# Half of the prompt's attention moved into the expert stage, and expert rows summed by token

## The reference, cut to what matters

```python
mod = (silu(c) @ w_ada + b_ada)              # shift, scale, gate of both halves
h   = rms(x, g_pre1) * (1 + sc1) + sh1
q, k, v, p = split(h @ w_in)                  # 8 heads of 64; p goes to a pooling group
# stick-breaking attention, strictly causal, for each query over its keys
log_1mb = where(mask, log_sigmoid(-z), 0)
after   = cumsum(log_1mb, reverse=True) - log_1mb
w       = where(mask, exp(log_sigmoid(z) + after), 0);  o_a = w @ v
x   = x + gt1 * rms(concat(rms(o_a), rms(o_b)) @ w_out)
h2  = rms(x, g_pre2) * (1 + sc2) + sh2
# experts: for each token and each of 8 heads
s1, s2 = the two halves of (h2 @ w_query) times 128 keys each
v1, i1 = top_k(s1, 16);  v2, i2 = top_k(s2, 16)
best, sel = top_k(all sums v1 + v2, 16);  idx = i1 * 128 + i2 at sel
act = gelu(h2 . u_tab[idx])                   # 128 rows of u for a token
x   = x + gt2 * rms(sum over the 128 of softmax(best) * act * v_tab[idx])
```

## Time and profile before

| | |
|---|---|
| median of 3 runs | 3820.96 us (3818.93 to 3822.36) |
| the profiled execution, first to last instruction | 4199.6 us |
| modulation and projection | 0 to 381 us |
| attention | 381 to 665.8 us |
| output | 665.8 to 904.6 us |
| experts, from the first gather | 904.6 to 4199.6 us |
| bytes moved | 1245.5 MB, 1141.0 of them gathered rows |

### The profile page before, as it was taken

How to read it: one execution, slowest core, us unless ns; L and a number is a source line. 1 busy time by engine, 2 the same in 40 slices (tenths; PEclk the granted TensorE clock), 3 DMA queues, 4 the chain that set the end, 5 groups by cost and what they waited for, 6 DMA issues and landing times.

```text
span 4199.6 us, 38180 instructions
## 1 busy us (share of the span) xinstructions
PE 3314.8 (79%) x9348; PEld 1593.5 (38%) x9348; DVE 2313.6 (55%) x5821; ACT 950.0 (23%) x2161; POOL 2152.0 (51%) x2222
## 2 busy tenths in 40 slices
PE   8998989928777777877777777777777777887677
PEld 2454555513333333333333333333333333333222
DVE  2104552867755665555665655566555665556442
ACT  1003773312221221112112211211121121112111
POOL 0000300236566665666666666566666665666665
PEclk9999999969898898898888888888888888888888
DMA  9104102159999999999999999899999999999997
GB/s 357 64 15 126 32 19 113 61 188 352 344 357 359 353 359 354 347 368 343 341 359 347 350 356 344 332 354 355 360 347 358 358 357 348 343 363 358 361 362 303
DMA packets 365168, 1245.51 MB, mean 297 GB/s; under 512 B 52129, under 2 KB 57505, under 8 KB 362751
## 3 DMA queue, kind: packets, MB, share of 16 engines
q0 software_dynamic: 313504, 1141.02, 72.4%
q1 hardware_dynamic: 48852, 96.77, 6.6%
q10 hardware_dynamic: 2576, 5.10, 0.4%
HBM read 1220.34 MB, written 22.39 MB: 296 GB/s over the span
## 4 chain that ended last, share of the span: by engine, by line
PE 38%; issue 17%; another core or an unknown queue 9%; DVE 5%; DMA 4%; POOL 3%; ACT 1%; DVEq 0%; POOLq 0%; ACTq 0%; SPq 0%
PE ps_y L1692 33%; PE ps_q L950 5%; DMA urow<-in_u_tab,idx 3%; POOL urow L1473 2%; POOL vrow L1473 1%; DMA vrow<-in_v_tab,idx 1%; DVE urow L1612 1%; ACT diag L1580 1%; DVE aux L993 0%; PE ps_s L961 0%; DVE i L996 0%; DVE sel L996 0%; DVE i L992 0%; DVE aux L1029 0%
## 5 line engine op out<-in xcount | busy, mean ns | idle before, releaser
L1692 PE MATMUL ps_y<-vrow,diag 128*128 128x512 f32 (+1 forms) x4352 | 2220.8, 665 | 647.5 <-issue 329.9
L1612 DVE CUSTOM_DVE_ANT_0 urow<-urow,ps_h 128x1024 f32<-128x1024 f32 x1088 | 1299.8, 1220 | 1025.2 <-DMA urow<-in_u_tab,idx 865.6
L1692 PEld LDWEIGHTS ps_y<-vrow,diag 128*128 128x128 f32 (+1 forms) x4352 | 884.3, 209 | 1893.6 <-issue 1576.9
L1473 POOL DMA_INDIRECT vrow<-in_v_tab,idx x1088 | 1031.6, 948 | 785.7 <-issue 287.4
L1473 POOL DMA_INDIRECT urow<-in_u_tab,idx x1088 | 1030.7, 947 | 430.5 <-issue 282.8
L1580 ACT ACTIVATE diag<-const,wgt 128x128 f32<-128x128 f32 x1024 | 373.1, 396 | 1766.2 <-PE ps_y L1692 643.3
L950 PE MATMUL ps_q<-aux,w_q_sb 128*128 128x128 f32 x2048 | 271.7, 292 | 58.1 <-issue 49.4
L950 PEld LDWEIGHTS ps_q<-aux,w_q_sb 128*128 128x128 f32 x2048 | 263.9, 207 | 94.4 <-issue 93.2
L1293 POOL TENSOR_TENSOR xo<-xo,ot 128x1024 f32<-128x1024 f32 (+1 forms) x9 | 21.1, 2343 | 352.2 <-DVE ot L1249 352.2
L530 PE MATMUL ps_z<-hT,w_in_sb 128*128 128x512 f32 (+1 forms) x576 | 190.5, 491 | 4.6 <-DVE hT L448 4.6
L625 POOL MEMSET kTs<- 128x384 f32 x1 | 0.4, 418 | 322.7 <-POOLq L344 322.7
(11 more groups left out here) (181 smaller groups left out, 2341.3 us busy)
## 6 DMA issues: line engine op xcount, KB each, us to landing
ada<-in_w_ada SPq DMA_DIRECT2D x12, 2048.0 KB, 12.5
urow<-in_u_tab,idx POOLq DMA_INDIRECT x1088
vrow<-in_v_tab,idx POOLq DMA_INDIRECT x1088
w_in_sb<-in_w_in SPq DMA_DIRECT2D x8, 1024.0 KB, 17.9
w_q_sb<-in_w_query SPq DMA_DIRECT2D x8, 1024.0 KB, 14.3
x<-in_x_p ACTq DMA_DIRECT2D x8, 512.0 KB, 6.6
w_out_sb<-in_w_out SPq DMA_DIRECT2D x8, 512.0 KB, 7.0
xo<-in_x_p SPq DMA_DIRECT2D x8, 512.0 KB, 3.7
```

Source lines behind the costliest of these rows:

```text
L1473: nc.gpsimd.indirect_dma_start(ring[k % RING][:, :], None, A[table][:, :], bass.IndirectOffsetOnAxis(ap=places[:, col:col + 1], axis=0)).t ...
L1612: nc.vector.tensor_tensor_reduce(out=urow[k % RING][:, :], in0=urow[k % RING][:, :], in1=ps_h[:, :], scale=1.0, scalar=0.0, op0=ALU.mult, ...
L1692: last = nc.tensor.matmul(ps_y[0:rows, c], diag[s % DIAGS][:, 0:rows], vrow[k % RING][:, c], start=(s == 0), stop=(s == PH * width(n) - 1))
```

## The change

1. The attention stage keeps tokens 0 to 511 and the sample: 11 units for a pair in place of 27. The output stage keeps the sample's tile and four tiles; the sample's searches stand at 2 and 3 and, five of them, among the last steps.
2. Tokens 512 to 1023 are done by a new class `Front` inside the expert stage, in 102 steps ("spots"): 72 of attention (4 pairs by 18 spots for 16 units: a spot gives PE the values, "after" and next scores of neighbouring units, ACT four functions, DVE softplus and R), the others the norm, the product with w_out, residual and second norm. They stand in bodies 1 (3 in a head), 2, 3 and the start of 4 (4 in a head), behind a quad on PE and behind every fourth product on DVE. K, V, q, x, w_out and the outputs go through DRAM once more, about 24.6 MB by the shapes in the code.
3. Ten bodies instead of nine: body b gathers u for tile b and v for tile b - 1, in turn. A v gather fetches all 128 rows of one token (`idxT`, the indices transposed). Four tokens make a quad: 8 products on PE, each 128 rows by 32 columns of weights (`place`, a window with the token's weights in one column) by 512, into four groups of 32 PSUM partitions. The 128x128 diagonals and their copies on ACT are gone. The u ring has 6 buffers (`URING`), the v ring 8.
4. The search is cut in 17 pieces, one behind each product, and is that of two heads ahead (`g + 2`); PE's queries and scores are three heads ahead. One bank of PSUM (`ps_find`) serves queries and scores.

Small edits in the first stages merge semaphores. The core of the diff:

```diff
-    for qc in range(2):
-        top = 4 * qc + 3
-        for kb in range(top, -1, -1):
-            c0 = max(0, kb * P - qc * 512)
-            for h in range(2):
-                units.append(dict(h=h, bank=qc, kb=kb, c0=c0, c1=512, first=kb == top, diag=kb >= 4 * qc,
-                                  last=kb == 0, opens=kb == top and h == 0, closes=kb == 0 and h == 1))
+    top = EARLY - 1
+    for kb in range(top, -1, -1):
+        for h in range(2):
+            units.append(dict(h=h, bank=0, kb=kb, c0=kb * P, c1=HALF, first=kb == top, diag=True,
+                              last=kb == 0, opens=kb == top and h == 0, closes=kb == 0 and h == 1))
     for kb in (2, 1, 0):
-        units.append(dict(h=2, bank=2, kb=kb, c0=0, c1=P, first=kb == 2, diag=kb == 2, last=kb == 0,
...
     NTILE = len(tiles)
...
-    heads = {2: [0], 3: [1], 4: [2], 5: [3], 6: [4], 7: [5], 8: [6, 7]}
...
-                for h in heads.get(t, []):
-                    find.search(own, dve, dve_passed, 0, h)
+                if t == 2:
+                    search(0)
+                if t == 3:
+                    search(1)
+                    search(2)
...
             second(NTILE - 3)
-            find.search(own, dve, dve_passed, 0, PH - 2)
+            search(3)
             product(NTILE - 1)
-            find.search(own, dve, dve_passed, 0, PH - 1)
             second(NTILE - 2)
+            search(4)
             residual(NTILE - 1)
+            search(5)
             second(NTILE - 1)
+            search(6)
+            search(7)
...
+    def unit(self, m):
+        j, h = divmod(m % self.UNITS, 2)
+        kb = NT - 1 - j
+        diag = kb >= EARLY
+        c0 = P * (kb - EARLY) if diag else 0
+        return m // self.UNITS, j, h, kb, diag, c0, (c0 + P if diag else 0)
+
...
+        self.nc.tensor.matmul(self.z[m % 2][:, c0:HALF], self.kT[hr, P * kb:P * (kb + 1)], self.q[hr, c0:HALF],
+                              start=True, stop=True, skip_group_check=True).then_inc(self.z_done, 1)
+
+    def after(self, pe, m):
+        i, j, h, kb, diag, c0, lo = self.unit(m)
+        z = self.z[m % 2]
+        pe.wait_ge(self.sp_done, m + 1)
+        last = self.nc.tensor.matmul(z[:, c0:HALF], self.ntri, self.sp[m % 2][:, c0:HALF], start=False, stop=True,
+                                     skip_group_check=True)
+        if j and lo < HALF:
+            last = self.nc.tensor.matmul(z[:, lo:HALF], self.nones, self.R[h][(j - 1) % 2][:, lo:HALF], start=False,
+                                         stop=True, skip_group_check=True)
...
+        i, j, h, kb, diag, c0, lo = self.unit(m)
+        nc, s = self.nc, self.sp[m % 2][:, c0:HALF]
+        act.wait_ge(self.z_done, m + 1)
+        if m >= 2:
+
+            act.wait_ge(self.t_done, m - 1)
+        own.link(nc.scalar.activation(s, self.z[m % 2][:, c0:HALF], ACT.Abs))
+        own.link(nc.scalar.activation(s, s, ACT.Exp, scale=-1.0))
...
+        i, j, h, kb, diag, c0, lo = self.unit(m)
+        act.wait_ge(self.t_done, m + 1)
...
+        self.nc.scalar.activation(self.w[m % 2][:, c0:HALF], self.z[m % 2][:, c0:HALF], ACT.Exp)\
+            .then_inc(self.e_done, 1)
...
+        dve.wait_ge(self.l_done, m + 1)
+        soft = nc.vector.scalar_tensor_tensor(out=s[:, c0:HALF], in0=self.z[m % 2][:, c0:HALF], scalar=0.0,
+                                              in1=s[:, c0:HALF], op0=ALU.max, op1=ALU.add)
+        if diag:
...
+            new, old = self.R[h][j % 2], self.R[h][(j - 1) % 2]
+            fresh = HALF if j == 0 else lo
+            if fresh > c0:
+                own.add(nc.vector.tensor_copy(new[:, c0:fresh], s[:, c0:fresh]))
+            if fresh < HALF:
+                own.add(nc.vector.tensor_tensor(new[:, fresh:HALF], old[:, fresh:HALF], s[:, fresh:HALF], ALU.add))
...
+        def spot(g, j):
+
+            if g < PH:
+                return None
+            if g < 2 * PH:
+                return 3 * (g - PH) + j - 1 if j else None
+            p = 3 * PH + 4 * (g - 2 * PH) + j
+            return p if p < front.END else None
...
+                k, at = v_slot(n, i) % VRING, find.idxT[n % 2][:, t:t + 1]
...
+                nc.gpsimd.indirect_dma_start(vrow[k][:, :], None, A["v_tab"][:, :],
+                                             bass.IndirectOffsetOnAxis(ap=at, axis=0)).then_inc(v_full[k], 16)
+
+            for b in range(BODIES):
+                nu = PH * width(b) if b < NU else 0
+                nv = rows(b - 1) if b else 0
+                for i in range(max(nu, nv)):
+                    if i < nu:
+                        gather_u(b, i)
+                    if b == 1:
+                        if i % 2:
+                            gather_v(0, i // 2)
+                    elif i < nv:
+                        gather_v(b - 1, i)
...
-                        products(un, uh)
...
-                        find.search(own, dve, dve_passed, n + 1, h - 1)
...
+                    for k in range(w):
...
+                        if k == (1 if h == 0 else 2) and g:
+                            weights(g - 1)
+                        if b == 0:
...
+                        if g + 2 < HEADS and k + early < find.STEPS:
+                            find.search(own, dve, g + 2, k + early)
...
+                        if k % 4 == 3 and spot(g, k // 4) is not None:
+                            front.on_dve(dve, own, spot(g, k // 4))
...
+            def quad(n, c):
...
+                pe.wait_ge(placed, n * QUADS + c + 1)
+                for i in range(j):
+                    s = v_slot(n, j * c + i)
+                    pe.wait_ge(v_full[s % VRING], 16 * (s // VRING + 1))
                 for half in range(2):
...
-            def add_row(n, h, k):
-                rows = DEC if is_sample(n) else P
-                s = width(n) * h + k
-                pe.wait_ge(v_full[k % RING], filled(n, h, k))
-                pe.wait_ge(diag_ready, slots(n, h) + (k + 1))
-                for half in range(2):
-                    c = slice(512 * half, 512 * (half + 1))
-                    last = nc.tensor.matmul(ps_y[0:rows, c], diag[s % DIAGS][:, 0:rows], vrow[k % RING][:, c],
-                                            start=(s == 0), stop=(s == PH * width(n) - 1))
-                last.then_inc(v_used, 1)
...
+                    cols = slice(512 * half, 512 * (half + 1))
+                    for i in range(j):
+                        s = v_slot(n, j * c + i)
+                        last = nc.tensor.matmul(ps_y[QUADS * i:QUADS * (i + 1), cols],
+                                                place[:, z, i, MID - c:MID - c + QUADS], vrow[s % VRING][:, cols],
+                                                start=(c == 0), stop=(c == QUADS - 1))
+                        if half:
+                            last.then_inc(v_used, 1)
...
-            run(pe, lambda: None, body, lambda: None)
+                    g = head(b, h)
...
+                    for j in range(4):
...
+                        quad(b - 1, 4 * h + j)
+                        if j == 3 and g + 3 < HEADS:
+                            find.scores(pe, g + 3)
+                        if spot(g, j) is not None:
+                            front.on_pe(pe, spot(g, j))
...
+                            if h3 == 0 and j in (1, 2):
...
+                                find.queries(pe, g + 3)
```

More of the change, by code:

```diff
@@ new lines, in take_places, with by_slot @@
+    def take_places(self, dve, n, bank, v_used):
+        nc = self.nc
+        dve.wait_ge(self.idxT_tr, n + 1)
+        if n >= 2:
+            dve.wait_ge(v_used, v_slot(n - 1, 0))
+        nc.vector.tensor_copy(self.idxT[n % 2][:, 0:rows(n)], bank[:, 0:rows(n)]).then_inc(self.idxT_ready, 1)
+def by_slot(nc, n, bank, c0, tile, ident):
+    if not is_sample(n):
+        return nc.tensor.transpose(bank[:, c0:c0 + P], tile[:, :], ident)
+    for half in range(2):
+        p = slice(DEC * half, DEC * (half + 1))
+        last = nc.tensor.matmul(bank[p, c0:c0 + DEC], tile[p, 0:DEC], ident[p, p], start=True, stop=True,
+                                skip_group_check=True)
+    return last
@@ L1263, in second, with search @@
                                                op0=ALU.mult, op1=ALU.mult).then_inc(x1_scaled, 1)
+            def search(h):
+                for step in range(find.STEPS):
+                    find.search(own, dve, h, step)
             dve.wait_ge(S["prepared"], KC + 6)
@@ L1351, in _ @@
                     last.then_inc(ab_done, 1)
-                    if half == 0:
-                        for h in heads.get(t, [])[:1]:
-                            find.scores(pe, 0, h)
-                        for h in heads.get(t, [])[1:]:
-                            find.queries(pe, 0, h)
-                for h in heads.get(t, [])[1:]:
-                    find.scores(pe, 0, h)
+                    if half == 0 and t in (2, 3):
+                        find.scores(pe, t - 2)
+                        if t == 3:
+                            find.queries(pe, 2)
```

(37 more changed lines are left out.)

1140 lines of the change are left out of this document (760 added, 380 removed).

## The result

The changed kernel takes **3784.97 us** (median of 4 runs, 3776.31 to 3787.60) against 3821.66 (4 runs): ratio 0.9899, 95% interval 0.9885 to 0.9913. It is faster, as forecast, but by 37 us where 171 were forecast (3650).

The account below looks back on a forecast made before the run. It took the expert stage as near DMA-bound, attention and output as engine chains. First gather 683, gather-paced terms 2,524 and other terms 443 gave 3650 us timed; range 3575 to 3795, leaving out the chain and the fastest end.

Parts of the forecast that it names:

- first gather: End of attention and output: the expert stage's first gather at 683 us in place of 904.6, 222 us less.
- body 0 with its start: Expert stage's start: 7.4 us from first gather to first product, then 108 for 64 DVE products, u gathers alone.
- body 1: Second body of the expert stage: 8 heads of products, search pieces and 3 spots each on DVE, 290 us.
- bodies 2 to 8: 1,792 gathers at 1.45 us, 2598 profiled, plus 62 for moved transfers and 27 for PE; 2381 timed.
- last u gather to the end: Last body: 128 v gathers alone, 32 quads of 6.0 us, 192 profiled (170 timed), then 11 for last quad and norm.
- rows no cheaper: Rival, gathers of bodies 2 to 8: 1.489 us each, no gain, 70 us more (62 timed), 3715 to 3720; chance 0.15.
- quads one after another: Rival, PE in the expert stage: a quad takes 7.08 us, its products not side by side, about 3795; chance 0.11.
- Attention and output: Front stages: attention ends at 491.6 us; output's searches and other work bring the first gather to 683.
- To timed runs: Profile's 378.6 us excess put wholly in the gather stage: gather-paced terms times 0.885, 2852 to 2524 us.
- PE's load and the moved transfers: Expert bodies: 27 us for PE's overloaded heads and moved output steps, 62 us for moved transfers in DMA-bound bodies.
- chain exposed: Rival: DVE waits in order for ACT at 72 attention spots, up to 5 us each, 3830 to 3990; chance 0.12.
- DVE frees a u buffer after each product: Bodies 2 to 8: a buffer freed every 1.94 us, two gathers needing 2.9, so POOL's blocked time goes in part.

Follow-up runs that it names:

- second profile: The kernel before, unchanged, profiled again: 3819.2 us in its one execution, against 4199.6 in the profile the prediction was made from.
- block run: The changed kernel with 14 of a search's 17 pieces in one block behind a head's 13th product, not one behind each product: 3823.80 us.

## Why the prediction was wrong in size

From the experiments the 37 us are a sum of steps from kernel to kernel: the restructured stage **+25** (3848.71 - 3823.61, the runs of before beside it), half of the front gone **-233** (3848.71 to 3615.26), its work put into the bodies **+170**. The forecast of faster was right for the front's sake alone. By its own steps:

| step | forecast, timed | measured |
|---|---|---|
| first gather | 683 | 669 |
| body 0 with its start | 115 | 103 |
| body 1 | 290 | 314 |
| bodies 2 to 8 | 2299 + 55 + 27 = 2381 | 2449 |
| last u gather to the end | 170 + 11 = 181 | 250 |
| sum | 3650 | 3785 |

Three steps failed: the end, 69 us too low; the price of a gather in bodies 2 to 8, 46; and the moved work, 46 (22 in bodies 2 to 8, 24 in body 1). The first two rows came out 26 lower than forecast. That 3785 lies inside the stated 3575 to 3795 is luck: the upper part of that range stood for rows no cheaper and for quads one after another, not for what failed here.

*Attention and output*: right, 14 us too high. *Body 0*: DVE-bound as said (busy for 59 of 60 us between 700 and 760), 12 too high.

*To timed runs*: this step failed first, and the price of a gather with it. That the excess lay in the gather stage was right: the front of the second profile is as long as that of the first. But the prediction read room for the gathers from an execution at 352 GB/s, took half of it as gain (1.489 to 1.45) and put that through the factor 0.885, which made a gather 1.283 us. It is 335 / 256 = 1.309, and was 1.330 before (340.5 / 256), both at a DMA share of 1.01 or 1.02. That is 46 of the 68 in bodies 2 to 8. The sign was in the prediction: it computed 391 GB/s for a timed run and had 352 in view, and used that only against a rival.

*Rivals*: "rows no cheaper" was nearest for the rows, 1.489 x 0.885 = 1.318. That the DMA path was full was right; the level it was full at, 352, was that one execution's. The 358 GB/s that the Trainium skill gives for a core (DMA: Bandwidth & Descriptors, Specifications) agrees with the 352 of the first profile, and not with the 396 to 409 of the later ones; the rate there decides.

*The end*: mis-sized by 69. I priced the last body by the pace of gathers, 6.0 us for a quad profiled, while my own count of the v ring (22 of 23 us) held only for v gathers that come every 2.9 us. With v alone POOL issues them every 1.245, and eight buffers give 14.17 us for two quads, 7.1 each. The run with 14 buffers shows it: 60 us off, and 193 from the last u gather to the end where the forecast had 181.

*PE's load and the moved transfers*: the transfers were sized right (62 profiled, 55 timed, 57 measured). The 27 for PE was wrong in kind: with quads side by side PE is busy for 236 of 372 us in body 2. What costs is the order: in-order PE holds a spot behind a quad that waits for rows, and ACT, DVE and the u ring wait in line. That is the rival "chain exposed" in part. Its sign came: DVE's wait ahead of softplus is 2.6 us each (168.5 / 64), over the 2.4 that was to show the forecast wrong. Its price came only in part: 113 us over 72 attention spots, 1.6 each. The prediction set it aside because a spot has 11.6 us to the next; it left out that PE reaches the spot only behind the quad's wait, 9.03 us in the row above.

*Quads one after another*: did not happen. The run that forces it is 178 above the change, where the rival had 145; the sum is near by luck, since the rival had 84 for all heads and 35 for the end, and the run has 133 in bodies 1 to 4 and 13 in the last. The Trainium skill (TensorE: Matmul & The Clock Gate, Part 3) has three column tiles at 2.38 times; the run has four at 3.67.

*"DVE frees a u buffer after each product"* as a reason for cheaper rows fell with the block run. Of the two blocked rows that it was read from in the earlier trace rows, the second, 3.83 us at 2330.73, is a v gather, which waits for PE to free a v buffer and not for a product.

## What to carry to other kernels

Put the rate and span of a profile beside the timed runs before a row is used as a price; where bytes over timed stage exceed the rate in view, take another profile. Work moved under a transfer-bound loop cost its bytes at the full rate here (57 us), and twice that again (113) where an in-order engine held it behind an operand that was still under way: put the work that is ready ahead of the wait (81 us). When two interleaved streams end apart, count the buffers of the last one for the time from its own issue to release: lend it those of the stream that is done (60 us).

## What was not expected of the hardware

One execution of the same program moved 352 GB/s and another 396 in the same stretch, the front stages alike (first gather 904.62 and 902.33). And PE's clock: with quads waiting for rows PE is busy for 151 of 335 us of a quiet body and its mean granted clock there is 0.66; a quad at 0.50 (1.2 GHz) takes 3.64 us against 1.92 at 1.00. In the kernel whose quads can't run side by side PE is busy for 280 of 341 us and the clock is 0.92:

```profile
2673.00:3014.00 341.00, 280.31 (x814) 90.66 (x813) 217.29 (x584) 39.10 (x83) 241.44 (x257) 0.92 1.01 398
```
